# Output projection w_o of a decoder layer: a new order of its 28 block products, of VectorE's work beside them, and of the squares for the next norm

## What is computed

```python
x = x + 0.5 * gate1(c) * SwiGLU_1(modulate(rms_norm(x)))
h = modulate(rms_norm(x))
y = (sigmoid(g_nsa) * (nsa(h) @ w_up_nsa) + sigmoid(g_fox) * (fox(h) @ w_up_fox)) @ w_o   # w_o is 1024 x 1024
x = x + gate2(c) * y
h = modulate(rms_norm(x))            # needs the sum of x*x over all features of a token
x = x + 0.5 * gate3(c) * SwiGLU_2(h)
out = rms_norm(x)
```

## Time and profile before

| | us |
|---|---|
| median of 3 runs (lowest, highest) | 2453.43 (2452.48, 2454.91) |
| the profiled execution's own time | 2450.02 |
| its span in the profile | 2448.1 |
| PE busy | 2316.3 (95%) |
| DVE, ACT, POOL busy | 1385.6 (57%), 1088.6 (44%), 1249.8 (51%) |
| mean granted clock of PE | 0.98 of full speed |

### The profile page before, as it was taken

How to read it: one execution, slowest core, us unless ns; L and a number is a source line. 1 busy time by engine, 2 the same in 40 slices (tenths; PEclk the granted TensorE clock), 3 DMA queues, 4 the chain that set the end, 5 groups by cost and what they waited for, 6 DMA issues and landing times. The chain is left out here.

```text
span 2448.1 us, 30080 instructions
## 1 busy us (share of the span) xinstructions
PE 2316.3 (95%) x10920; PEld 1884.8 (77%) x10920; DVE 1385.6 (57%) x1664; ACT 1088.6 (44%) x2060; POOL 1249.8 (51%) x967
## 2 busy tenths in 40 slices
PE   4999999999999899999799999999789999999997
PEld 2788888888877777788677877777578888888885
DVE  5846555266557755742588888575463323225554
ACT  4533333323445443333688888423543333323332
POOL 3454444445564555444557545355745555435473
PEclk7999999999999999999899999999999999999998
DMA  6155544265451433343803046323212222245362
GB/s 254 59 185 176 189 174 160 75 227 168 151 168 48 142 120 128 143 170 129 248 14 88 18 110 173 105 93 130 94 53 85 83 82 94 73 169 175 116 188 88
DMA packets 128946, 314.98 MB, mean 129 GB/s; under 512 B 13408, under 2 KB 34016, under 8 KB 128800
## 3 DMA queue, kind: packets, MB, share of 16 engines
q1 hardware_dynamic: 127824, 310.76, 38.5%
q10 hardware_dynamic: 976, 2.29, 0.4%
HBM read 241.51 MB, written 69.34 MB: 127 GB/s over the span
## 5 line engine op out<-in xcount | busy, mean ns | idle before, releaser
L1635 POOL TENSOR_TENSOR r_z<-f_main,r_z 128x512 fp32r<-128x512 f32 x254 | 353.4, 1394 | 394.3 <-ACT r_z L1031 394.1
L2536 PE MATMUL ps<-r_main,r_z 128*128 128x512 f32 x1232 | 483.7, 393 | 21.4 <-issue 13.4
L2537 PE MATMUL ps<-r_main,r_z 128*128 128x512 f32 x1232 | 481.7, 391 | 0.0
L2538 PE MATMUL ps<-r_main,r_z 128*128 128x512 f32 x1232 | 481.4, 391 | 0.0
L1641 POOL TENSOR_TENSOR r_main<-f_main,r_main 128x1024 fp32r<-128x1024 f32 x88 | 217.0, 2469 | 221.3 <-ACT r_main L1072 221.3
L2536 PEld LDWEIGHTS ps<-r_main,r_z 128*128 128x128 f32 x1232 | 232.8, 189 | 71.3 <-issue 23.0
L2512 PE MATMUL ps<-r_main 128*128 128x512 f32 x688 | 269.0, 391 | 3.4 <-DVE r_main L1998 3.4
L2538 PEld LDWEIGHTS ps<-r_main,r_z 128*128 128x128 f32 x1232 | 232.8, 189 | 48.9
L2537 PEld LDWEIGHTS ps<-r_main,r_z 128*128 128x128 f32 x1232 | 232.9, 189 | 48.7 <-issue 0.2
L2514 PE MATMUL ps<-r_main 128*128 128x512 f32 x688 | 267.8, 389 | 0.0
L2513 PE MATMUL ps<-r_main 128*128 128x512 f32 x688 | 267.7, 389 | 0.0
(11 more groups left out here) (309 smaller groups left out, 4626.8 us busy)
## 6 DMA issues: line engine op xcount, KB each, us to landing
f_main<-in_wd SPq DMA_DIRECT2D x88, 512.0 KB, 3.7
f_main<-in_w_ada SPq DMA_DIRECT2D x56, 512.0 KB, 5.1
act_d<-f_main SPq DMA_DIRECT2D x88, 256.0 KB, 2.0
f_main<-act_d SPq DMA_DIRECT2D x88, 256.0 KB, 3.8
f_main<-in_wg SPq DMA_DIRECT2D x20, 1024.0 KB, 5.0
f_main<-in_wu SPq DMA_DIRECT2D x20, 1024.0 KB, 5.1
f_main<-in_wmix SPq DMA_DIRECT2D x18, 1024.0 KB, 5.3
r_main<-qk_hi_d SPq DMA_DIRECT2D x40, 256.0 KB, 7.1
```

The lines of the kernel that those rows point to most:

```text
L1635: pool.tensor_tensor(prod_lo_t[slot], source_of(g), prod_hi_t[slot].bitcast(F32), ALU.subtract).then_inc(s["wl"], 1)
L2536: pe.matmul(out, wh, hi, start=start, stop=False, skip_group_check=True)
L2537: pe.matmul(out, wh, lo, start=False, stop=False, skip_group_check=True)
L2538: return pe.matmul(out, wl, hi, start=False, stop=stop, skip_group_check=True)
```

## The change

The order of the 28 products: for the first two pairs the products alternate between the pairs (from g = 2 on: (0,7) (0,6) (1,7) (1,6) (0,2) (1,2) (0,5) (1,5) (0,4) (1,4) (0,3) (1,3)), and the last four become (2,5) (3,5) (2,3) (3,3). The ring of five weight tiles serves only g = 0 to 14; g = 15 to 23 use a ring of three (tiles 30, 31 and f_main tile 13). So the three tiles that hold the square buffers are free after g = 14, and squares and their sums are placed between the products, from step 13 on ACT, 17 on POOL and 18 on DVE. DVE's work at the start is reordered, and ACT, POOL and DVE get new orders at the end; `std(2, 0)` moves behind the first two weight casts of SwiGLU_2.

The diff, cut to its core (`O_SPLITS` becomes `O_HIGHS` and `O_LOWS`, and waits that count these are renamed with them):

```diff
-O_ORDER = ([(0, 1), (1, 1)] + [(0, q) for q in (7, 6, 2, 5, 4, 3)] + [(1, q) for q in (7, 6, 2, 5, 4, 3)]
-           + [(u, q) for u in (2, 3) for q in (1, 7, 6, 2, 4)] + [(u, q) for u in (2, 3) for q in (5, 3)])
+O_ORDER = ([(u, 1) for u in (0, 1)] + [(u, q) for u in (0, 1) for q in (7, 6)] + [(u, q) for q in (2, 5, 4, 3) for u in (0, 1)]
+           + [(u, q) for u in (2, 3) for q in (1, 7, 6, 2, 4)] + [(u, q) for q in (5, 3) for u in (2, 3)])
 O_AT = {e: g for g, e in enumerate(O_ORDER)}
-O_RING, O_LATE = 5, 24
-O_SPLITS = ([(q, i) for i in range(4) for q in (1, 5)] + [(q, i) for q in (7, 6, 2) for i in range(3)] + [(q, 3) for q in (7, 6, 2)]
-            + [(q, i) for q in (4, 3) for i in range(4)])
-O_SPLIT_AT = {e: k + 1 for k, e in enumerate(O_SPLITS)}
+O_PIECE = {2: (0, 0), 4: (1, 0), 5: (1, 1), 3: (0, 1)}
+O_ADDS = [[2 * u + O_PIECE[q][0] for u, q in O_ORDER if q in O_PIECE and O_PIECE[q][1] == h] for h in range(2)]
+O_LATE = 24
+O_TILE = [(32, 33, 34, 30, 31)[g % 5] for g in range(15)] + [None, 30, 31] * 3 + [4, 5, 6, 7]
+O_TILE_BEFORE = [max((j for j in range(g) if O_TILE[j] == O_TILE[g]), default=None) for g in range(O_LATE)] + [O_AT[3, 1]] * 4
+O_WEIGHT_STEP = {13: [16], 14: [17], 15: [18], 16: [19], 17: [20], 18: [21], 19: [22], 20: [23, 24], 21: [25, 26], 22: [27],
+                 **{g: [g + 5] for g in range(5, 11)}}
+O_HIGHS = ([(q, i) for i in range(4) for q in (1, 5)] + [(q, i) for q in (7, 6, 2) for i in range(3)] + [(q, 3) for q in (7, 6, 2)]
+           + [(q, i) for q in (3, 4) for i in range(4)])
+O_HIGH_AT = {e: k + 1 for k, e in enumerate(O_HIGHS)}
+O_LOWS = ([(q, i) for i in range(4) for q in (1, 5)] + [(q, i) for q in (7, 6) for i in range(3)] + [(7, 3), (6, 3)]
+          + [(q, i) for q in (2, 4, 3) for i in range(4)])
+O_LOW_AT = {e: k + 1 for k, e in enumerate(O_LOWS)}
+O_SQ = [0, 1, 2, 3, 8, 9, 10, 11, 4, 5, 6, 7, 13, 15, 12, 14]
+O_SQ_STEP = {13: (0, 1), 14: (2,), 15: (3,), 16: (8,), 17: (9,), 18: (10,), 19: (11,), 20: (4,), 21: (5,), 22: (6,), 23: (7,)}
+O_SUM_P = [1, 2, 3, 5, 13]
+O_SUM_D = [9, 10, 11, 6, 7, 12, 14]
+O_SUM_OF = {0: 1, 4: 6, 8: 9, 15: 12}
+SUM_P = (0, 0, 8, 8 + len(O_SUM_P))
+SUM_D = (0, 0, 4, 4 + len(O_SUM_D))
 O_XSUMS = [(1, i) for i in range(4)] + [(n, i) for i in range(4) for n in (3, 2)] + [(4, i) for i in range(4)]
 O_XSUM_AT = {e: k + 1 for k, e in enumerate(O_XSUMS)}
-O_WSUMS = [(0, 3), (0, 1), (0, 2), (0, 4), (1, 3), (1, 1), (1, 2), (1, 4), (2, 3), (2, 1), (2, 2), (3, 3), (3, 1), (2, 4), (3, 2), (3, 4)]
+O_WSUMS = [(0, 3), (0, 1), (0, 2), (1, 3), (1, 1), (1, 2), (0, 4), (1, 4), (2, 3), (2, 1), (2, 2), (3, 3), (3, 1), (2, 4), (3, 2), (3, 4)]
 O_WSUM_AT = {e: k + 1 for k, e in enumerate(O_WSUMS)}
-O_WSUM_STEP = {1: [(0, 4)], 2: [(1, 3), (1, 1)], 3: [(1, 2)], 7: [(1, 4)], 9: [(2, 3), (2, 1)], 11: [(2, 2)], 13: [(3, 3), (3, 1)], 14: [(2, 4)],
-               16: [(3, 2)], 19: [(3, 4)]}
+O_WSUM_STEP = {9: [(2, 3), (2, 1)], 11: [(2, 2)], 13: [(3, 3), (3, 1)], 16: [(2, 4)], 17: [(3, 2)], 20: [(3, 4)]}
...
-        o_slot = [rt((32, 33, 34, 30, 31)[g % O_RING] if g < O_LATE else 4 + g - O_LATE) for g in range(len(O_ORDER))]
+        o_slot = [r_f[:, 13 * KW:14 * KW] if a is None else rt(a) for a in O_TILE]
...
         def o_weight_free(e, g):
 
-            if g >= O_LATE:
-                e.wait_ge(osem["mm"], O_AT[3, 1] + 1)
-            elif g >= O_RING:
-                e.wait_ge(osem["mm"], g - O_RING + 1)
+            if O_TILE_BEFORE[g] is not None:
+                e.wait_ge(osem["mm"], O_TILE_BEFORE[g] + 1)
-            return n + 1 if h == 0 else (n ^ 1) + 1
+            return O_ADDS[h].index(n) + 1
...
         def square_used(e, k, j):
 
             h, n = divmod(j, NT)
-            if n in (4, 6, 7):
-                e.wait_ge(nsem["sd"], 4 * (k - 1) + 2 * h + (2 if n == 7 else 1))
+            if k == 2:
+                j = O_SUM_OF.get(j, j)
+                sums, name = (O_SUM_P, "sp") if j in O_SUM_P else (O_SUM_D, "sd")
+                e.wait_ge(nsem[name], (SUM_P if j in O_SUM_P else SUM_D)[k] + sums.index(j) + 1)
+            elif n in (4, 6, 7):
+                e.wait_ge(nsem["sd"], SUM_D[k] + 2 * h + (2 if n == 7 else 1))
             else:
-                e.wait_ge(nsem["sp"], 8 * (k - 1) + 4 * h + (0, 0, 1, 2, 0, 3)[n] + 1)
+                e.wait_ge(nsem["sp"], SUM_P[k] + 4 * h + (0, 0, 1, 2, 0, 3)[n] + 1)
...
+            def out_square(j):
+
+                at = O_SQ.index(j)
+                act.wait_ge(o_x[j // NT], o_added(j % NT, j // NT))
+                if at >= 3:
+                    square_used(act, 2, O_SQ[at - 3])
+                act.activation(sq_f[at % 3], x[:, j % NT, halves(j // NT)], ACT.Square).then_inc(nsem["sq"], 1)
 
...
             for q in (7, 6, 2):
                 for i in range(3):
                     out_x_high(q, i)
-            for g in (3, 4):
-                out_weight_high(g)
+            out_weight_high(3)
             out_taken(0)
             for q in (7, 6, 2):
                 out_x_high(q, 3)
+            out_weight_high(4)
             out_taken(1)
             out_weight_high(5)
+            out_taken(2)
+            for i in range(4):
+                out_x_high(3, i)
             out_weight_high(6)
+            out_weight_high(7)
+            out_taken(4)
             for i in range(4):
                 out_x_high(4, i)
-            for g in range(2, O_LATE):
+            out_weight_high(8)
+            out_weight_high(9)
+            for g in range(5, O_LATE):
                 out_taken(g)
-                if 7 <= g + O_RING < O_LATE:
-                    out_weight_high(g + O_RING)
-                if g in (2, 3):
-                    out_x_high(3, 2 * g - 4)
-                    out_x_high(3, 2 * g - 3)
-                if g == 19:
-                    for late in range(O_LATE, len(O_ORDER)):
-                        out_weight_high(late)
+                for later in O_WEIGHT_STEP.get(g, ()):
+                    out_weight_high(later)
+                for j in O_SQ_STEP.get(g, ()):
+                    out_square(j)
                 if g == 20:
                     root_table()
-                    act.wait_ge(osem["mm"], O_AT[3, 2] + 1)
-                if g >= 21:
-                    for j in {21: (0, 1, 2), 22: (3, 4, 5), 23: (6, 7)}[g]:
-                        square(2, j, out_added)
+            for g in range(2):
+                weight_high(1, g)
             std(2, 0)
-            for g in range(4):
+            for g in range(2, 4):
                 weight_high(1, g)
-            for j in range(8, 14):
-                square(2, j, out_added)
+            for j in (13, 15):
+                out_square(j)
             shifted(2, 0)
-            for m in range(2):
-                shifted(2, m + 1)
-                if m == 0:
-                    act.wait_ge(osem["mm"], O_LATE)
-                x_high(2, 1, m)
-            for j in (14, 15):
-                square(2, j, out_added)
+            out_square(12)
+            shifted(2, 1)
+            act.wait_ge(osem["mm"], O_LATE)
+            x_high(2, 1, 0)
+            shifted(2, 2)
+            x_high(2, 1, 1)
+            out_square(14)
             for m in range(2, 4):
                 shifted(2, m + 1)
                 x_high(2, 1, m)
...
+            def out_square_sum(j):
+
+                s, h, before = nsem, j // NT, O_SUM_P.index(j)
+                pool.wait_ge(s["sq"], SQ[2] + O_SQ.index(j) + 1)
+                if j == 13:
+                    pool.wait_ge(s["sd"], SUM_D[2] + O_SUM_D.index(11) + 1)
+                elif before > 0:
+                    pool.wait_ge(s["sp"], SUM_P[2] + before)
+                square = sq_f[O_SQ.index(j) % 3]
+                pool.tensor_tensor(sum_p[h], sq_f[O_SQ.index(0) % 3] if j == 1 else sum_p[h], square, ALU.add).then_inc(s["sp"], 1)
...
                     out_weight_low(m - 4)
             for g in range(3, len(O_ORDER)):
                 out_weight_low(g)
-            for n in POOL_SUMS:
-                square_sum(2, n)
-            for g in range(4):
+                if g in (17, 18, 19, 23):
+                    out_square_sum({17: 1, 18: 2, 19: 3, 23: 5}[g])
+            for g in range(2):
                 weight_low(1, g)
-            for n in POOL_SUMS:
-                square_sum(2, NT + n)
+            out_square_sum(13)
+            for g in range(2, 4):
+                weight_low(1, g)
             scaled_x(2, 0)
...
+            def out_square_sum(j):
+
+                s, at = nsem, O_SUM_D.index(j)
+                dve.wait_ge(s["sq"], SQ[2] + max(O_SQ.index(j), O_SQ.index({9: 8, 6: 4, 12: 15}.get(j, j))) + 1)
+                total, square = sum_p[1] if j in (9, 10, 11) else sum_d, sq_f[O_SQ.index(j) % 3]
+                if j in (9, 6, 12):
+                    if j == 12:
+                        dve.wait_ge(s["mm"], 2 * 2 + 1)
```

(80 more changed lines are left out.)

2 lines of the change are left out of this document (removed).

## The result

| | before | after |
|---|---|---|
| median (lowest, highest), us | 2453.03 (2451.39, 2454.91) | 2440.20 (2436.54, 2441.78) |
| ratio, 95% interval | | 0.9945 [0.9935, 0.9956] |
| span in the profile, us | 2448.1 | 2438.5 |
| PE busy, us | 2316.3 | 2313.8 |
| first product of w_o to the end of the span, us | 805.7 | 795.4 |

The kernel is 12.8 us faster by the medians, where 13.4 was forecast. The profiled executions differ by less, 9.6 us in their spans, and that is the difference that can be followed place by place.

What follows compares the result with a forecast made beforehand. PE, 95% busy, bounds the kernel, so time is won only where it stands still. Gains of 5.9 us up to g = 24 and 7.3 at the seam make 13.2, taking 2453.4 to 2440 us; range 2435 to 2449.

Steps and rivals of the forecast that it cites:

- Head: Part 1, w_o's products g = 0 to 13: the stall at (0,7) goes, a smaller one comes at g = 12.
- 28 operations: DVE's queue from 1648.7 to the end of c22(0), ahead of g = 12: forecast to take 28.6 us.
- the 2.4 us: PE's forecast stall ahead of g = 12, waiting for DVE's c22(0); bounds 0 and 4.
- price of 1.1 us per POOL operation: Delay to DVE's low parts before c22(0) from each POOL operation beside them; eleven make 12.1 us.
- the clock at g = 12: Loss to half clock after the g = 12 stall: 0.8 us, half of 1.6; bounds 0 and 3.0.
- Ring of three: Part 2, g = 15 to 23: zero cost, a turn taking 4.7 us at worst of the 5.44 available.
- the throttle rival: In g = 15 to 23 PE waits in every product and the kernel is slower, 2458 at 2 us each; 5%.
- Seam: Part 3, from g = 24's end to SwiGLU_2's second group: 24.4 us against 31.7, 7.3 gained; bounds 5.0 and 9.0.
- E: The end of product g = 24: forecast at 1713.6, 5.9 us earlier than 1719.5.
- The sum: Whole gain up to SwiGLU_2's second group: 5.9 + 7.3 = 13.2 us, against the profiled execution.
- the rival in which the clock falls: At g = 12 half clock costs 3.0 us, not 0.8: gain 11.0, 2442.4 us; 20%.
- without contention: If POOL did not slow DVE, the g = 12 stall would be 0 and the gain 2.4 us larger.

Runs made afterwards that it cites:

- tail_order: The changed kernel with the last four products back in the old order, squares 12 and 15 exchanged to match: 2441.06 us, ratio 0.9955 to the kernel before.
- after_again: The changed kernel run once more with no edit: 2441.74 us, ratio 0.9952 to the kernel before.
- std_first: The changed kernel with std(2, 0) back ahead of SwiGLU_2's first two weight casts on ACT: 2437.91 us, ratio 0.9945 to the kernel before.
- weights_later: The changed kernel with ACT's weight casts 10 to 15 moved to later steps, a void edit (same moment in the run): 2442.15 us, ratio 0.9957 to before.
- head_only: The kernel before with only the new start (first two pairs alternating, DVE's and ACT's orders there), old ring and seam: 2447.93 us, ratio 0.9984 to before.
- sum5_last: The changed kernel with POOL's square sum 5 behind low parts 24 to 27 instead of ahead: 2436.36 us, ratio 0.9935 to the kernel before.

## Why the prediction was right, and where it was not

**Head.** The wait at (0,7) and its half clock are gone. DVE's difference of x ends at T + 6.35, as forecast; its 28 operations took until T + 35.75, 29.4 us where 28.6 were forecast; PE took up g = 12 at T + 35.85 (forecast 35.0). Though DVE is 0.8 late, the gap is 2.12 and not more, because PE came late too, mainly from the 0.62 us wait for wl(8): "what they lose is paid out of the 2.4 us". The price of 1.1 us per POOL operation holds: in the block above nine SBUF operations of DVE take 13.1 us, by the earlier trace rows about 5.6 alone, so 7.5 for seven POOL operations. All eleven in the stretch cost 11.8 us, where the forecast had 12.1 less 0.6 for one hidden behind PSUM operations: that is 0.3 of the 0.8. The other 0.5 are small delays between operations, which I had put at 0.61 from start to start throughout; three weight sums start 0.71 and 0.80 apart:

```profile
1650.73 0.68 DVE L2458 TENSOR_TENSOR s<-f_main 128x512 f32<-128x512 f32 x1
1651.44 0.69 DVE L2461 TENSOR_TENSOR f_main<-f_main 128x512 f32<-128x512 f32 x1
1652.24 1.79 DVE L2465 TENSOR_TENSOR f_main<-f_main 128x512 f32<-128x512 f32 x1
```

**The mis-sized term is the clock at g = 12.** I took 0.8 us. From T + 35.85 to the end of g = 24 at T + 73.0 are 37.1 us for 13 products that need 35.4: 1.8 lost. The rows after the stall show it, matmuls 0.427 apart (the 1.2 GHz level) for 3.4 us:

```profile
1679.47 0.44 PE L2928 MATMUL ps<-r_main,r_z 128*128 128x512 f32 x1
1679.71 0.63 PE L2926 MATMUL ps<-r_main,r_z 128*128 128x512 f32 x1
1680.13 0.63 PE L2927 MATMUL ps<-r_main,r_z 128*128 128x512 f32 x1
...
1683.11 0.39 PE L2928 MATMUL ps<-r_main,r_z 128*128 128x512 f32 x1
```

So the head gained 4.1 us, not 5.9 (0.8 for DVE, 1.0 for the clock). The forecast was an even chance of full or half clock, and this is what the runs show: of seven profiled executions with this stall (2.12 or 2.13 us, in tail_order 2.11) the clock fell in four (after, after_again, std_first, weights_later) and not in three (head_only, sum5_last, tail_order). The windows from T + 35.8 to T + 41.5 of after and of tail_order (us, busy time of each engine, granted clock, DMA share, GB/s):

```profile
1678.90:1684.60 5.70, 5.67 (x18) 4.60 (x19) 5.53 (x9) 0.62 (x1) 1.29 (x1) 0.70 1.00 399
```

```profile
1681.30:1687.00 5.70, 5.67 (x25) 4.71 (x26) 5.53 (x9) 0.62 (x1) 1.29 (x1) 1.00 0.99 389
```

18 matmuls in the one, 25 in the other. stat(2, 0) stands at T + 73.7 or 73.8 where it fell and at T + 72.1 or 72.2 in sum5_last and tail_order: 1.6 us. The forecast's half of that fits these seven as a mean; that this profile had the slow case is chance.

**Ring of three.** No gap from g = 14 to 23, as forecast: cost zero, the throttle rival is out. ACT's table load and what POOL does behind it:

```profile
1707.47 1.28 ACT L999 ACT_TABLE_LOAD   x1
1708.76 0.21 ACT L999 ACTIVATE warm<-eps 128x1 f32<-128x1 f32 x1
...
1710.61 1.30 POOL L1643 TENSOR_TENSOR f_z<-f_z 128x512 f32<-128x512 f32 x1 [2.84 <-ACT f_z L1017]
1711.86 1.29 POOL L1774 TENSOR_TENSOR r_main<-f_z,r_main 128x512 fp32r<-128x512 f32 x1
```

The low part of g = 24 ends at 1713.15 and PE begins that product at 1713.25: 0.1 to spare, as forecast. ScalarE: Activation LUTs in the Trainium skill, section What ACT_TABLE_LOAD costs, gives about 1283 ns for the load and, with a drain of 1380 ns, 2.66 us for a switch. The load takes 1.28 here as well. But it starts 0.02 behind the end of ACT's instruction before it, and the next one starts 0.01 behind the load, so the trace does not show the drain, and g = 24 was not late.

**Seam**, from E = 1716.07. ACT, then POOL:

```profile
1721.79 1.14 ACT L1056 CAST r_z<-f_main 128x512 fp32r<-128x512 f32 x2 [6.11 <-DMA f_main<-in_wg]
1722.84 0.68 ACT L1022 ACTIVATE f_main<-ps,eps 128x512 f32<-128x512 f32 x1
...
1716.07 1.71 POOL L1774 TENSOR_TENSOR r_main<-f_main,r_main 128x512 fp32r<-128x512 f32 x1
1722.49 2.53 POOL L1668 TENSOR_TENSOR r_z<-f_main,r_z 128x512 fp32r<-128x512 f32 x2 [4.71 <-ACT r_z L1056]
1725.28 1.26 POOL L1643 TENSOR_TENSOR f_z<-f_z 128x512 f32<-128x512 f32 x1 [0.26 <-ACT f_z L1017]
1726.50 2.96 POOL L1668 TENSOR_TENSOR r_z<-f_main,r_z 128x512 fp32r<-128x512 f32 x2
1729.43 6.66 POOL L1663 TENSOR_TENSOR f_main<-f_main 128x512 f32<-128x512 f32 x5
```

| from E, us | forecast | measured |
|---|---|---|
| stat(2, 0) waits | 0.8 | 0.6 |
| gate rows issued | 1.9 | 1.7 |
| first cast | 5.4 | 5.7 |
| std | 6.5 | 6.8 |
| wait ahead of g = 27, its end | 3.3, 11.3 | 3.4, 11.5 |
| scaling | 12.6 | 13.4 |
| first group of SwiGLU_2 | 18.4 | 19.1 |
| second group | 24.4 | 26.0 (24.8 and 24.7 in after_again and weights_later) |

The order of events is right in each step. 0.8 us is missing up to the scaling: the first cast came 0.3 later (the load landed 4.0 us after its issue, not 3.5), square sum 13 waited 0.26, and the second pair of low parts took 2.96. The other 0.9 lies between the two groups: the 12 matmuls of the first ran at half clock behind waits of 3.4 and 3.1 us (5.3 us up to stat), and stat itself took 1.6. That part belongs to this execution: in after_again and weights_later the first group starts at E + 19.2 too, but only about half of it runs at half clock, and the second group comes at E + 24.8 and 24.7. So the seam gained 5.7 us here and 6.9 to 7.0 there, against 7.3: the size was off, not the mechanism. std_first shows that the stall ahead of g = 27 isn't what counts, and sum5_last that the end moves with the gate rows.

**The sum** was 13.2 us against the profiled execution; the traces show 9.8 at the second group, in the two repeats 11.1. The forecast still met the median of its set of runs, since the two medians lie 3 us further apart than the two profiled executions: that before's profiled execution was a quick one (2450.02, below the lowest of its timed runs, 2451.39) made up for terms that were too large. With after_again and weights_later the change is worth 10.5 to 13.5 us by the ratios. So the mechanism was right, and that 2440 was met to 0.2 us is luck: the terms behind it were 2.1 to 3.4 us too large against the traces, and the 11.0 us of the rival in which the clock falls is nearer to them. Three small slips stand in the prediction's sums: 1677.3 less 1675.0 is 2.3, not 2.4; nine products at 1.5 us are 13.5, not 13.2; and without contention the gain would be larger by 3.2, since the 0.8 for the clock would go with the stall.

## What to carry to other kernels

Follow the wait at a seam back to the first transfer: here the next stage's first weight load hung on the last low part of this one, and one square sum moved behind four low parts was worth about 4 us. When two elementwise engines share a critical stretch, count the other engine's operations in it, and move either the operation that someone waits for to the front, or the ones that nobody waits for to the back. A stall made on an engine beside that chain (3.4 us ahead of g = 27) cost nothing that could be seen: with it removed, the first group came 0.5 us earlier and the ratio stayed within its interval.
